# A chunked recurrence: token rows of the scaled keys and removal vectors by VectorE's 32x32 transposes and DMAs instead of by TensorE

## What is computed

```python
def wkv_scan(r, w, k, v, a, b, s0, reverse):
    def step(S, xs):
        r_t, w_t, k_t, v_t, a_t, b_t = xs
        sa = jnp.einsum('bhvk,bhk->bhv', S, a_t)
        S = S * w_t[:, :, None, :] + sa[..., None] * b_t[:, :, None, :] + v_t[..., None] * k_t[:, :, None, :]
        return S, jnp.einsum('bhvk,bhk->bhv', S, r_t)
    xs = tuple(jnp.swapaxes(t, 0, 1) for t in (r, w, k, v, a, b))
    s_T, o = lax.scan(step, s0.astype(jnp.float32), xs, reverse=reverse)
    return jnp.swapaxes(o, 0, 1), s_T
```

## Time and profile before

| | us |
|---|---|
| median of 3 runs | 2950.79 |
| their range | 2949.8 to 2956.48 |
| the profiled execution | 2945.5 |
| its span | 2943.8 |
| TensorE busy | 2691.4 (91%) |
| VectorE busy | 1306.2 (44%) |
| ScalarE busy | 558.2 (19%) |
| GpSimd busy | 485.5 (16%) |

### The profile page before, as it was taken

One profiled execution on the slowest core, in us unless ns is written; L12 is line 12 of the kernel. 1 busy time (PEld: TensorE's weight loads), 2 busy tenths in 40 slices (PEclk: granted clock), 3 DMA queues, 4 the chain that ended last, 5 costly groups with the idle time before them and its releaser, 6 DMA issues. The chain is left out here.

```text
span 2943.8 us, 60987 instructions
## 1 busy us (share of the span) xinstructions
PE 2691.4 (91%) x26020; PEld 1538.1 (52%) x26020; DVE 1306.2 (44%) x2324; ACT 558.2 (19%) x1552; POOL 485.5 (16%) x654
## 2 busy tenths in 40 slices
PE   5699989999979599999889999999999999999996
PEld 1367767666657589998744444333333333333332
DVE  1667576676626466665323114422233232222333
ACT  2100011022005355555422111100000000000002
POOL 0104000000015466675131000000000000000000
PEclk8899999999989789999989999999999999999998
DMA  9567555544627312211098878899999999999999
GB/s 408 223 211 212 191 171 196 215 179 179 220 63 154 134 40 48 68 49 45 21 355 339 306 291 341 314 400 403 403 403 404 404 399 394 401 404 405 405 413 353
DMA packets 263749, 777.50 MB, mean 264 GB/s; under 512 B 99986, under 2 KB 161065, under 8 KB 195329
## 3 DMA queue, kind: packets, MB, share of 16 engines
q1 hardware_dynamic: 251216, 712.63, 64.2%
q0 software_dynamic: 11968, 61.92, 7.0%
q10 hardware_dynamic: 368, 0.10, 0.0%
HBM read 707.81 MB, written 66.77 MB: 263 GB/s over the span
## 5 line engine op out<-in xcount | busy, mean ns | idle before, releaser
L2276 PE MATMUL oe_ps<-experts_ring,tail_arena 128*32 128x512 f32 x4096 | 500.2, 603 | 43.2 <-DMA experts_ring<-in_w_up 43.1
L620 DVE SCALAR_TENSOR_TENSOR pj_macc<-pj_mring,head_cond_t,pj_macc 128x1024 f32<-128x1024 f32 x240 | 297.0, 1278 | 186.5 <-DMA pj_mring<-in_w_ada 186.5
L2276 PEld LDWEIGHTS oe_ps<-experts_ring,tail_arena 128*32 128x32 f32 x4096 | 150.7, 111 | 341.2 <-issue 340.1
L732 PE MATMUL pj_ps<-head_hT,head_ring_in 128*128 128x320 f32 x1104 | 312.1, 436 | 6.6 <-DVE head_hT L593 4.2
L2309 PE MATMUL oe_ps<-experts_ring,oe_hidt 128*32 128x512 f32 x2880 | 312.0, 592 | 0.0
L2284 PE MATMUL oe_ps<-experts_ring,tail_arena 128*32 128x512 f32 x2048 | 272.2, 598 | 0.0
L732 PEld LDWEIGHTS pj_ps<-head_hT,head_ring_in 128*128 128x128 f32 x1104 | 210.8, 191 | 96.0 <-DVE head_hT L593 6.6
L2648 DVE SCALAR_TENSOR_TENSOR oe_hid_s<-oe_hid_s,oe_gcol_s,oe_ps 128x512 f32<-128x512 f32 x16 | 12.0, 747 | 534.6 <-ACT oe_hid_s L2490 534.6
L2381 PE MATMUL oe_ps<-experts_ring,tail_arena 128*128 128x512 f32 x480 | 220.8, 609 | 17.4 <-DMA experts_ring<-in_w_out 12.9
L732 PE MATMUL pj_ps<-pj_t,pj_s 128*128 128x320 f32 x736 | 210.3, 439 | 7.0 <-DVE pj_t L599 7.0
L2309 PEld LDWEIGHTS oe_ps<-experts_ring,oe_hidt 128*32 128x32 f32 x2880 | 108.0, 110 | 201.0 <-issue 201.0
(11 more groups left out here) (414 smaller groups left out, 3952.7 us busy)
## 6 DMA issues: line engine op xcount, KB each, us to landing
experts_ring<-in_w_gate SPq DMA_DIRECT2D x128, 1024.0 KB, 23.9
experts_ring<-in_w_up SPq DMA_DIRECT2D x128, 1024.0 KB, 26.2
experts_ring<-in_w_down SPq DMA_DIRECT2D x128, 1024.0 KB, 22.6
experts_ring<-in_w_out SPq DMA_DIRECT2D x68, 1024.0 KB, 7.3
pj_mring<-in_w_ada SPq DMA_DIRECT2D x64, 1024.0 KB, 9.7
head_ring_in<-in_w_in SPq DMA_DIRECT2D x23, 2048.0 KB, 8.5
ada_ring<-in_w_ada SPq DMA_DIRECT2D x16, 2048.0 KB, 19.5
scratch_z<-pj_stage POOLq DMA_DIRECT2D x19, 640.0 KB, 8.0
```

What stands on the lines that cost most here:

```text
L620: a = nc.vector.scalar_tensor_tensor(acc, w, scalar, acc, ALU.mult, ALU.add)
L732: mm = pe.matmul(bank(name, b)[:, 0:TH], a[:, k, :], h[:, k, :], start=(k == 0), stop=(k == KH - 1))
L2276: pe.matmul(ps[32 * i:32 * i + 32, bank, :], xe[:, k, GROUPS[i % 2]], w[:, kk * DE + 512 * (i // 2):kk * DE + 512 * (i // 2) + 512], start ...
```

## The change

The three jobs "bk" and ScalarE's copies are gone. In their place stand two items of VectorE, "flip0" (behind d(0,2), for the removal vectors) and "flip1" (behind x(0,3), for the keys); the place of the third is left empty. Each flip transposes 32x32 blocks of ten chunk tiles in two instructions of 128x320 and writes them to the new tensor `flips`. A 64x64 tile is then turned only within its four 32x32 blocks, and the blocks have to change places across partitions: SP does this with eight DMAs of 80 KB per unit (`swap_blocks`), issued behind `blocks_back`. Their rows are contiguous, 32 x 20 numbers, because `bktok` now has the chunk as its innermost index. So the stationary operand of one chunk is read with a step of 20 numbers (80 bytes). The flips of unit u wait for the swap of unit u-1, since `flips` has one buffer, and the first "pw" of a unit waits for its swap instead of for ScalarE's last copy.

```diff
@@ plan @@
-        bk = [("bk", b, u) if now else None for b in range(3)]
-                 lv["d", 0, 2], bk[0], "slot", lv["d", 1, 2], "slot", "exp_in", lv["x", 0, 3], bk[1], "slot", lv["x", 1, 3], "exp_inv", "slot", "pad_b", lv["d", 0, 3], bk[2], "slot", "half0",
+                 lv["d", 0, 2], "flip0", "slot", lv["d", 1, 2], "slot", "exp_in", lv["x", 0, 3], "flip1", "slot", lv["x", 1, 3], "exp_inv", "slot", "pad_b", lv["d", 0, 3], "slot", "half0",
@@ tensors @@
-        bktok = sb("bktok", [P, NS, 2 * NCK, DH])
+        bktok, flips = sb("bktok", [P, NS, DH, 2 * NCK]), sb("flips", [P, 2, HB, 2 * NCK])
+        MADE, SWAPS = 1, 8 * 16
@@ sync @@
+            def swap_blocks(u):
+
+                sp.wait_ge(flipped, 2 * (u + 1))
+                for h in range(2):
+                    for n in range(2):
+                        for m in range(2):
+                            sp.dma_start(bktok[DH * h + HB * m:DH * h + HB * m + HB, u % NS, HB * n:HB * n + HB], flips[DH * h + HB * n:DH * h + HB * n + HB, m]).then_inc(swapped, 16)
                 blocks_out(u)
                 blocks_back(u)
+                swap_blocks(u)
@@ tensor, run_job @@
-                elif kind == "bk":
-                    pe.wait_ge(bkp_done, 2 * u + 2)
-                    for i in range(min(8, 2 * NCK - 8 * b)):
-                        mm = heads(bank[:, i * DH:(i + 1) * DH], bk[:, u % 2, 8 * b + i, :], eye[:], True, True)
@@ tensor, stage @@
-                        emptied([("bk", 2, v), ("vt", 1, v - v % 2), ("sc", NCK // 2 - 1, v)])
+                        pe.wait_ge(swapped, SWAPS * (v + 1))
+                        emptied([("vt", 1, v - v % 2), ("sc", NCK // 2 - 1, v)])
-                        heads(zv, bktok[:, n, NCK + c, :], vk, True, False, skip_group_check=True)
+                        heads(zv, bktok[:, n, :, NCK + c], vk, True, False, skip_group_check=True)
-                        heads(zv, bktok[:, n, c, :], usb[:, k, :], False, True, skip_group_check=True)
+                        heads(zv, bktok[:, n, :, c], usb[:, k, :], False, True, skip_group_check=True)
@@ scalar, empty @@
-                elif kind == "bk":
-                    m = min(8, 2 * NCK - 8 * b)
-                    a = nc.scalar.copy(bktok[:, u % NS, 8 * b:8 * b + m, :].rearrange("p c k -> p (c k)"), bank[:, 0:m * DH])
@@ vector @@
+            def flip(u, which):
+
+                dve.wait_ge(bkp_done, 2 * u + which + 1)
+                if which == 0 and u:
+                    dve.wait_ge(swapped, SWAPS * u)
+                cols = slice(which * NCK, which * NCK + NCK)
+                for n in range(2):
+                    f = nc.vector.transpose(flips[:, n, :, cols].rearrange("p i c -> p c i"), bk[:, u % 2, cols, HB * n:HB * n + HB])
+                f.then_inc(flipped, 1)
```

More of the change, by code:

```diff
@@ L1169, in kept_items @@
         if u >= NU:
-            skip |= {"half0", "half1", "far"}
+            skip |= {"half0", "half1", "far", "flip0", "flip1"}
         return [i for i in items if i is not None and i not in skip]
@@ L1205, in on_act @@
     def on_act(key):
-        return key[0] in ("w", "a", "s0", "vt", "bk")
+        return key[0] in ("w", "a", "s0", "vt")
     RANK = [sum(on_act(m) == on_act(key) for m in JOBS[:g + 1]) + on_act(key) for g, key in enumerate(JOBS)]
@@ L1251, in block_rwkv @@
             ("wd", "we", "ud", "ue", "zd", "oe", "sr"))
-        shifted = sem("shifted")
+        shifted, flipped, swapped = sem("shifted"), sem("flipped"), sem("swapped")
         fo_out, osum_done, o_out = sem("foout"), sem("osum"), sem("oout")
@@ L1255, in block_rwkv @@
         NLOAD, NLOADW = 4 * 16, 6 * 16
-        MADE = 1
+        MADE, SWAPS = 1, 8 * 16
         def ready(v, i):
@@ L1766, in _ @@
                         removal(u + 1)
+                    elif item in ("flip0", "flip1"):
+                        flip(u, int(item[-1]))
                     elif item in ("pad_b", "pad_k"):
```

## The result

The changed kernel takes 2980.53 us (median; 2976.53 to 2984.76), against 2950.30 for the kernel before on the same chip: ratio 1.0101, 95% interval [1.0075, 1.0128], 30 us slower. The forecast was 2937 us within 2922 to 2967. The profiled execution is the slowest of the four, 2984.76 us (span 2983.0), 39 above the one of before.

A forecast was written before the change was run, and what follows sets the result against it. TensorE was taken to set the lines' pace. A line gains 2.0 us, loading lines lose 0.4: seven keep 11.2, lines 14 and 15 keep 4.0, the earliest loses 1; 14 us in all, 2937 us by the median, range 2922 to 2967.

The forecast's parts named there:

- VectorE's path from R: VectorE's work from removal on, flips included: 4.7 us against 6.24 before, so a line gains 2.0 us in all.
- R: The start of VectorE's "removal" in a line, 1243.12 us in line 9; forecast 0.4 us late in loading lines.
- SyncE's eight issues: Swap issues ahead of the next pair's loads: 3.8 us (2.7 to 5.1), removal 0.4 us late in loading lines.
- the strided reads: TensorE's stationary operand bktok read every 80 bytes: taken as costing nothing, at most 2.1 us a line if doubled.
- TensorE's jobs, 38.6 us: Three removed bk jobs, 2.41 us for 80 records in each of 16 lines: 38.6 us, the most to be won.
- The rival with the whole gain: Load lands in time and VectorE's holes take the flips: 30 to 36 us won, 2918 us, chance 0.09.
- The turns, 505 ns: Each of VectorE's four 128x320 transposes per line: 505 ns taken, the near end, against 833 at the other.
- the far end: The costly estimate: 833 ns per turn by doubled slope; for strided reads, each column twice as long, 2.1 us a line.
- the reduction: VectorE row over 256 elements 64 bytes apart, 581 ns, 1.7 ns per element; gave 833 ns for a turn, set aside.
- The even and the slower rival: Even: only strided reads or only flips slow, 2950 or 2947 us, chance 0.22; slower: both, 2967 us, chance 0.22.
- The first rival: Strided columns cost double on TensorE and in VectorE's transposes: 16 us slower, 2967 us, chance 0.22.
- The rival given 0.03: The wait on the swap binds, or flips displace a state update in a second place: a few us slower.

The follow-up runs named there:

- e12: Changed kernel without the eight swaps and without strided reads, so only VectorE's turns are added (TensorE reads zeros): 2946.7 us, ratio to before 1.0004.
- e13: Changed kernel without VectorE's turns and without strided reads, so only SyncE's eight swaps are added (carrying zeros): 2959.6 us, ratio to before 1.0044.
- e7: The ceiling: kernel before without the bk jobs and ScalarE's copies, nothing in their place (bktok holds zeros): 2920.7 us, ratio to before 0.9905.
- e3: As e0 (turns read zeros), and the turns write 32 neighbours while TensorE still reads with the stride: 2966.9 us, ratio to before 1.0063.
- e14: Changed kernel without VectorE's turns and without the eight swaps, so only the strided reads (of zeros) are added: 2930.7 us, ratio to before 0.9941.
- e5: Changed kernel without both strides (turns and reads), turns and swaps kept in their places, transfers in runs of 128 bytes: 2969.3 us, ratio to before 1.0076.
- e8: Changed kernel with the turns at the head of the line and SyncE's loads ahead of the swaps, both strides kept: 2934.9 us, ratio to before 0.9959.
- e1: As e0 (turns read zeros), and TensorE reads 64 neighbours instead of with the stride: 2978.7 us, ratio to before 1.0104.
- e2: Kernel before with bktok in the changed layout: ScalarE writes it and TensorE reads it with the stride, jobs and copies stay: 2967.5 us, ratio 1.0071.
- e10: As e8 (turns at the line's head, loads first, strides kept), with the scores ahead of the swaps: 2936.0 us, ratio to before 0.9956.
- e0: Changed kernel whose turns read a tile of zeros instead of bk, all instructions, waits and transfers kept: 2979.6 us, ratio to before 1.0128.
- e4: Changed kernel with only SyncE's order changed: loads, the last unit's swap, scores, weights: 2965.2 us, ratio to before 1.0051.
- e6: As e8 (turns at the line's head, loads ahead of swaps), without strides, as in e5's layout: 2938.0 us, ratio to before 0.9968.
- e11: As e6 (turns at the line's head, loads first, no strides), with the scores ahead of the swaps: 2922.1 us, ratio to before 0.9917.
- e9: Changed kernel with only the turns moved to the head of the line, ahead of the scan, SyncE's order kept: 3088.0 us, ratio to before 1.0478.

## Why the prediction was wrong

A gain of 14 us was forecast and 30 us were lost. Two terms of the sum failed. VectorE's path from R was to leave 2.0 us a line, but the turns alone cost 29 us (e12), all of the saving. SyncE's eight issues were to make R 0.4 us late in a loading line, but alone they cost 41 us (e13). A third was put at nothing and costs 11 us alone, the strided reads. And one step was missing: that the new waits take TensorE's clock down.

- **TensorE's jobs, 38.6 us: right as busy time, 8 to 11 us too large as time.** e7 shows 38.8 us of busy time and 28 us of the median. The rival with the whole gain, 30 to 36 us, lay at or above what can be had with nothing in the place of the jobs.
- **The turns, 505 ns: wrong end of the bracket.** They take 839, and the far end, 833, was right, in part by luck: the reduction's slope was 1.7 times a transpose's, and the prediction rounded that to double. With neighbours e3 has 469, near the 505. The reduction's row was set aside as ambiguous, though it was the only one with a stride near that of the change (64 bytes read, against 80 written).
- **VectorE's path from R: right in kind.** 4.7 us were forecast with fast turns and 6.0 with slow ones; from 1289.90 to 1295.49 it measures 5.6, against 6.24. The prediction had TensorE wait 0.4 us a line for st; it waits 1.0. The wait was also counted at its own length alone, see the points on the clock.
- **SyncE's eight issues, 3.8 us (2.7 to 5.1): undersized.** In the line at 1243 they take 5.0, in others up to 6.6, with single issues up to 1.9, and kk is issued 8.1 us behind comp where it was 1.8. That is 6.3 us later instead of 3.8; 1.2 of it is the first load's own issue, 1.54 us behind the eight where it took 0.34. In four of the seven loading lines "removal" then waits for kk, 5.9, 0.7, 3.5 and 1.5 us, and not 0.4 in each; in the others, that at 1243 among them, the slack still covers it. The prediction took kk's own 0.43 us as the price, though the same queue's row showed 0.59 for the state load; the swaps measure 0.591.

```profile
1243.13 0.34 SPq L1304 DMA_DIRECT2D rw_comp<-scratch_tb  x1
1243.52 5.02 SPq L1312 DMA_DIRECT2D rw_bktok<-rw_flips  x8
...
1251.24 0.43 SPq L1272 DMA_DIRECT2D rw_kk<-scratch_kk  x1
```

- **The strided reads, nothing: wrong.** The load goes from 135 to 200 ns and a group of four from 0.12 to 0.26 us (1264.47 to 1264.73 is all at the upper level), so the far end's doubling was right per record, at that level. On the whole kernel it is 11 us (e14: 24.1 us busy, of which 12.4 fill idle time), not the 34 of 16 x 2.1, in part because the slower groups also take up waits that the shorter program has.

  The Trainium skill's "Advanced Engine Details and Errata", section SBUF Cachelines, said that accesses must hit a 16-byte line twice to hide its latency, and the trace agrees in three places: loads 200 against 135 ns, turns 839 against 469, ScalarE's copies 1222 against 585, all with one number every 80 bytes against neighbours; no run has another stride. It gives no size. The reads are the smallest of the three causes.
- **The even and the slower rival.** The first rival, slower at 2967 with both strides double, named the right sign, with 0.22. But its mechanism isn't what decides: without both strides (e5) the kernel takes 2969, and with both, moved (e8), 2935. The rival given 0.03, flips that displace a state update at a few us, was the nearest to the truth in kind, though much too small.
- **What no step had: the clock.** The prediction wrote the granted clock down as 1.00 and never asked what the new waits would do to it. Against the ceiling the changed kernel's TensorE is busy 57.3 us more in the recurrence (457.1 - 399.8). The reads are 24.1 of these (e14 - e7); the other 33 come with 81 us more at the lower level, which can cost 40. Idle time adds 9.7. Three kernels price the clock by itself, since they have e7's 10666 records and its loads of 135 ns: e12, e13 and e1 are busy 16.9, 9.1 and 44.2 us more than e7 with 32, 23 and 111 us more at the lower level, 0.4 to 0.5 each. So in the profiled execution, the slowest of its four, the largest of the terms is work done at half the rate. No experiment holds the clock up with the waits in place, so this share is read from the traces and not shown by a run.
- **What brings the falls is settled only in part.** Between 1060 and 1440 us, before, e2, e8, e10 and e14 have no wait of TensorE of 0.8 us or more, and at most 7 us at the lower level from 115 us behind the first scan on (the fall in which each recurrence ends isn't counted). The kernels with 9 to 15 such waits (after, e0, e1, e4, e5, e6, e12, e13) have 10 to 82 there. But e7 and e11 have 7 and 5 waits of up to 1.9 us, and 0 and 3 us; e9 has eleven of 8 to 12 us, and 97; e3 has three, and 61, and its clock fell for 17 us at 1142.6 behind waits of only 0.58 and 0.55. Waits go with the falls; neither their number nor their length foretells how much is lost.

## What to carry to other kernels

Ask of a step moved off the bounding engine first what stands behind it on its new queue, and for a DMA what its issues delay: here three parts of the change worth 11, 29 and 41 us alone undid a saving of 28, and two changes of order (turns at the head of the line, ahead of the scan; swaps behind the loads and the scores) and a layout without strides brought back nearly all of it. Move both ends together: with a single buffer, a producer that is moved forward waits for the consumer that was left late (e9, 141 us slower than before). On a TensorE that is kept at full clock, a new wait may cost more than its own length: read PEclk behind it.

## What the runs showed of the hardware

- The granted clock fell from 2.4 to 1.2 GHz behind single waits of 1.0 us in an otherwise busy TensorE (1263.43 to 1264.47 above), stayed there 13.7 us and came back; other waits of that length had none behind them (1295.49), and kernels without waits of 0.8 us or more had 0 to 7 us at the lower level in the middle of the recurrence. In e3 it fell for 17 us behind waits of 0.58 and 0.55.
- The stationary operand of 64 float32 columns, one number every 80 bytes: 200 ns a load against 135, and 0.26 against 0.12 us for four records at the upper level.
- A 32x32 transpose of 128x320 on VectorE takes 839 ns when it writes every 80 bytes, 469 with neighbours. ScalarE's copy of 128x512, written so: 1222 against 585.
- An issue on SyncE of a transfer of 32 rows of 2560 bytes takes 591 ns at the median, and 648 with runs of 128 bytes; eight of them hold the queue for 5.0 to 6.6 us in the changed kernel.
